# Second block's output projection as seven block products, its two weight tiles released one after the other

## The reference, cut to what matters

```python
mixed = concatenate([rms_norm(out_a, ...), rms_norm(out_b, ...), rms_norm(out_c, ...)], axis=-1)
x = x + einsum('bsc,cd->bsd', mixed, w_out)              # 256x1024 by 1024x1024
x = x + expert_choice_moe(rms_norm(x, norm_ffn), w_router, b_router, w_gate, w_up, w_down)
...
# expert_choice_moe
logits = einsum('bsd,de->bse', x, w_router) + b_router
aff = softmax(logits)
gate, idx = top_k(aff.transpose(0, 2, 1), cap)
xs = x[bidx, idx]
hid = silu(einsum('becd,edf->becf', xs, w_gate)) * einsum('becd,edf->becf', xs, w_up)
ys = einsum('becf,efd->becd', hid, w_down) * gate
```

## Time and profile before

| | us |
|---|---|
| median of 3 runs | 1926.46 (1926.03 to 1927.03) |
| the profiled execution | 1926.92 |
| its span, first to last instruction | 1925.1 |
| PE busy | 1643.8 (85%) |
| DVE / ACT / POOL busy | 764.6 / 313.8 / 182.2 |
| bytes read from HBM | 594.76 MB |

### The profile page before, as it was taken

How to read it: one execution, slowest core, us unless ns; L and a number is a source line. 1 busy time by engine, 2 the same in 40 slices (tenths; PEclk the granted TensorE clock), 3 DMA queues, 4 the chain that set the end, 5 groups by cost and what they waited for, 6 DMA issues and landing times.

```text
span 1925.1 us, 25329 instructions
## 1 busy us (share of the span) xinstructions
PE 1643.8 (85%) x10768; PEld 941.6 (49%) x10768; DVE 764.6 (40%) x1502; ACT 313.8 (16%) x823; POOL 182.2 (9%) x175
## 2 busy tenths in 40 slices
PE   8999999999999999999776766757999785756757
PEld 3455999444589964574332232322474432232322
DVE  1586788877738886663010100102573010010101
ACT  1243111021521101262000000001252000010000
POOL 0001034000215410310000000000210000000000
PEclk9999999999999999999897987879999897897978
DMA  9992998434454743546999999999746999999998
GB/s 356 330 355 91 330 334 279 153 131 175 135 189 169 263 153 125 184 181 274 415 432 428 427 434 423 434 428 402 243 175 255 403 428 432 425 434 425 432 429 351
DMA packets 165960, 599.81 MB, mean 312 GB/s; under 512 B 20976, under 2 KB 79856, under 8 KB 142064
## 3 DMA queue, kind: packets, MB, share of 16 engines
q1 hardware_dynamic: 165630, 598.04, 79.2%
q10 hardware_dynamic: 242, 0.53, 0.1%
HBM read 594.76 MB, written 3.80 MB: 311 GB/s over the span
## 4 chain that ended last, share of the span: by engine, by line
PE 55%; DMA 38%; DVE 4%; ACT 2%; issue 1%; POOL 0%; SPq 0%; DVEq 0%; ACTq 0%; POOLq 0%
DMA extra<-in_w_down 14%; DMA extra<-in_w_up 13%; DMA extra<-in_w_gate 11%; PE ps L1393 7%; PE ps L1420 7%; PE ps L1747 5%; PE ps L1347 5%; PE ps L1018 4%; PE ps L1187 4%; PE ps L1464 4%; PE ps L1629 3%; PE ps L1289 3%; PE ps L1495 2%; PE ps L1767 1%; DVE extra L2548 1%
## 5 line engine op out<-in xcount | busy, mean ns | idle before, releaser
L1747 PE MATMUL ps<-ring,wide 128*32 128x256 f32 x2912 | 226.2, 478 | 123.9 <-DMA ring<-in_w_up 79.4
L1747 PEld LDWEIGHTS ps<-ring,wide 128*32 128x32 f32 x2912 | 109.5, 136 | 233.9 <-DMA ring<-in_w_up 89.0
L3446 DVE TENSOR_TENSOR wide<-ps,wide 128x512 f32<-128x512 f32 x16 | 10.7, 670 | 506.1 <-PE ps L1747 506.1
L1767 PE MATMUL ps<-ring,wide 128*32 128x512 f32 x768 | 158.4, 641 | 47.7 <-DMA ring<-in_w_down 44.0
L1747 PE MATMUL ps<-extra,wide 128*32 128x256 f32 x1056 | 87.1, 499 | 55.9 <-DMA extra<-in_w_up 31.8
L1767 PEld LDWEIGHTS ps<-ring,wide 128*32 128x32 f32 x768 | 42.2, 117 | 159.8 <-issue 127.6
L1393 PE MATMUL ps<-hT,ring 128*128 128x128 f32 x960 | 114.7, 275 | 0.0
L1393 PEld LDWEIGHTS ps<-hT,ring 128*128 128x128 f32 x960 | 111.0, 192 | 1.0 <-issue 1.0
L1347 PE MATMUL ps<-hT,ring 128*128 128x128 f32 (+1 forms) x704 | 100.2, 304 | 0.0
L2315 ACT ACTIVATE wide<-ps 128x512 f32<-128x512 f32 x8 | 4.8, 597 | 566.5 <-PE ps L1767 425.3
L1347 PEld LDWEIGHTS ps<-hT,ring 128*128 128x128 f32 x704 | 94.0, 191 | 5.8 <-issue 1.0
(11 more groups left out here) (399 smaller groups left out, 2364.5 us busy)
## 6 DMA issues: line engine op xcount, KB each, us to landing
ring<-in_w_gate SPq DMA_DIRECT2D x24, 4096.0 KB, 31.3
ring<-in_w_down SPq DMA_DIRECT2D x24, 4096.0 KB, 33.2
ring<-in_w_up SPq DMA_DIRECT2D x20, 4096.0 KB, 32.7
ring<-in_w_mod SPq DMA_DIRECT2D x24, 2048.0 KB, 12.9
ring<-in_w_up SPq DMA_DIRECT2D x44, 1024.0 KB, 9.5
extra<-in_w_gate SPq DMA_DIRECT2D x8, 4096.0 KB, 35.1
extra<-in_w_up SPq DMA_DIRECT2D x8, 4096.0 KB, 33.0
ring<-in_w_in SPq DMA_DIRECT2D x13, 2048.0 KB, 9.8
```

Of the source, the lines that this page charges most:

```text
L1747: last = mm(ps[2 * part + e // 2][j * CAP:(j + 1) * CAP, e % 2 * 2 * P:(e % 2 + 1) * 2 * P], xsT[:, k, e * CAP:(e + 1) * CAP], expert_row( ...
L1767: last = mm(ps[6 + n][e * CAP:(e + 1) * CAP, :], hidT[:, e, k, :], expert_row(n0, e, k)[:, n * N:(n + 1) * N], start=k == 0, stop=k == KD - 1)
```

## The change: what it does

The product `mixed @ w_out` is cut in two by rows (`c`), by the inner dimension (`e`, four of the eight chunks each) and by columns (`n`). Eight products of such blocks become seven, of four matmuls each: `block_out(m)`, in the order 1, 7, 2, 6, 3, 5, 4. For them DVE forms four sums of row blocks (`rows3`: s1 to s4, 512 elements a row) and four of weight blocks in place (`weights3`: t1 to t4, 2048 elements a row), and adds the products into `x` in more steps (`product_add`, `shared_add`). ACT copies product 1 once into `out2_u`. The rows of `w_out` are laid in another order in memory outside of the launch, to match `h8`. The far scale moves: DVE scales `proj2` itself (`far_scale`) ahead of the far transposes, and PE waits for that (`b2_mixed_ready`, 2). Row chunk 1 of `x` is now completed right half first. The weight tiles change places, ("out", 1) comes first; it is released by the first matmul of product 5, ("out", 0) by the last of product 4. The pair in their place is loaded as two halves (`pair_half`), each behind its own tile.

```diff
+OUT2_STEPS = (1, 7, 2, 6, 3, 5, 4)
+OUT2_BANK = {1: 4, 7: 5, 2: 2, 6: 0, 3: 1, 5: 3, 4: 6}
+OUT2_SUMS = ("s3", "t3", "t2", "s1", "s2", "s4", "t4", "t1")
+OUT2_NEEDS = {1: (), 7: ("s3", "t3"), 2: (), 6: ("s2", "t2"), 3: ("s4",), 5: ("s1", "t1"), 4: ("t4",)}
...
-B2_TILES = [("in", i) for i in range(5)] + [("small", 0), ("out", 0), ("out", 1)]
+B2_TILES = [("in", i) for i in range(5)] + [("small", 0), ("out", 1), ("out", 0)]
...
-                sp.wait_ge(tile_done, b2_used(L, 7))
-                pair(3)
+                for h in range(2):
+                    sp.wait_ge(tile_done, b2_used(L, SLOTS + h))
+                    pair_half(G_PAIRS - 1, h)
...
+                def block_out(m, some=range(4)):
+
+                    if some[0] == 0:
+                        for name in OUT2_NEEDS[m]:
+                            pe.wait_ge(*out2_sum(s, name))
+                    w, h = out2_weights(), out2_rows()
+                    lhs, rhs = {1: (h[0][0], w[0][0]), 2: (h[0][1], w[1][0]), 3: (h[0][1], w[1][1]), 4: (h[1][1], w[1][0]),
+                                5: (h[1][0], w[0][0]), 6: (h[0][0], w[0][0]), 7: (out2_s3, w[0][1])}[m]
+                    for g in some:
+                        last = mm(ps[OUT2_BANK[m]][:, :], lhs[:, g, :], rhs[:, g, :], start=g == 0, stop=g == 3)
+                        if m == 5 and g == 0:
+                            last.then_inc(tile_done, 1)
+                    if some[-1] == 3:
+                        if m == 4:
+                            last.then_inc(tile_done, 1)
+                        else:
+                            last.then_inc(s.up("block_product_done"), 1)
...
+                block_out(1)
+                block_out(7, range(0, 2))
+                pe.wait_ge(*s.at("b2_mixed_ready", 2))
                 for i, (_, _, col) in enumerate(FAR):
                     for c in range(2):
                         o = ((i + 1) % 2) * T + c * P
                         last = nc.tensor.transpose(ps[6 + (i + 1) // 2][:, o:o + P], proj2[:, c, col:col + P], ident)
                     if i in (0, 2):
                         last.then_inc(s.up("b2_out_flipped"), 1)
-                out2(5, NEAR, 0, 1).then_inc(s.up("b2_out_done"), 1)
-                out2(0, NEAR, 1, 0).then_inc(s.up("b2_out_done"), 1)
-                out2(1, NEAR, 1, 1).then_inc(s.up("b2_out_done"), 1)
+                block_out(7, range(2, 4))
+                pe.wait_ge(*s.at("b2_proj_by_act", 7))
                 pe.wait_ge(*s.at("b2_out_by_act", 3))
                 pe.wait_ge(*s.at("b2_out_by_dve", 2))
-                out2(2, FAR, 0, 0).then_inc(s.up("b2_out_done"), 1)
-                out2(3, FAR, 0, 1).then_inc(s.up("b2_out_done"), 1)
+                block_out(2)
+                block_out(6)
+                block_out(3)
...
-                out2(6, FAR, 1, 0, slice(0, 2))
-                flip_rows(0)
-                out2(6, FAR, 1, 0, slice(2, 3)).then_inc(tile_done, 1)
-                out2(7, FAR, 1, 1, slice(0, 2))
+                flip_rows(0, (0,))
+                block_out(5)
+                block_out(4, range(0, 2))
+                flip_rows(0, (1,))
+                block_out(4, range(2, 4))
                 pe.wait_ge(sems["router_loaded"], 16 + DEPTH)
                 pe.wait_ge(sems["pads_cleared"], 4)
                 pe.wait_ge(*s.at("b2_x_by_act", 3))
                 pe.wait_ge(*s.at("b2_x_by_dve", 3))
                 route(0).then_inc(s.up("b2_router_done"), 1)
-                out2(7, FAR, 1, 1, slice(2, 3)).then_inc(tile_done, 1)
+                flip_rows(1, (1,))
+                logits(0)
                 flip_rows(1, (0,))
-                logits(0)
-                flip_rows(1, (1,))
+                pe.wait_ge(*s.at("b2_x_by_act", 4))
+                route(1, range(4, KD), 1)
                 pe.wait_ge(*s.at("b2_x_by_dve", 4))
-                route(1, range(0, 4))
-                pe.wait_ge(*s.at("b2_x_by_act", 4))
-                route(1, range(4, KD)).then_inc(s.up("b2_router_done"), 1)
+                route(1, range(0, 4), 1).then_inc(s.up("b2_router_done"), 1)
...
+                act.wait_ge(*out2_done(s, L, 1))
+                av(out2_u, ps[OUT2_BANK[1]][:, :], ACT.Copy).then_inc(s.up("b2_proj_by_act"), 1)
...
+                def far_scale():
+
+                    dve.wait_ge(*s.at("b2_mixed_rstd", 2))
+                    for c in range(2):
+                        v = proj2[:, c, CQ2:CQ2 + 384]
+                        ts(v, v, rsm[1][:, 3 * c + 2:3 * c + 3], None, ALU.mult)\
+                            .then_inc(s.up("b2_mixed_ready" if c else None), 1)
+
+                def rows3(name):
+
+                    if name == "s3":
+                        dve.wait_ge(*s.at("b2_out_by_act", 2))
+                    elif name == "s1":
+                        dve.wait_ge(*s.at("b2_out_by_act", 3))
                     else:
-                        dve.wait_ge(tile_done, b2_used(L, B2_AT[("out", n)]))
-                    xv = x[:, c, n * N:(n + 1) * N]
-                    stt(xv, ps[2 + 4 * c + n][:, :], rsm[1][:, 3 * c + 2:3 * c + 3], xv, ALU.mult, ALU.add)\
-                        .then_inc(s.up("b2_mixer_added"), 1)
+                        dve.wait_ge(*out2_done(s, L, {"s2": 1, "s4": 2}[name]))
+                    dve.wait_ge(*s.own())
+                    out_, p, q, op = {"s3": (out2_s3, h[0][0], h[1][0], ALU.subtract), "s1": (h[1][0], h[1][0], h[1][1], ALU.add),
+                                      "s2": (h[0][0], h[1][0], h[0][0], ALU.subtract),
+                                      "s4": (h[0][1], h[0][1], h[0][0], ALU.subtract)}[name]
+                    tt(out_, p, q, op).then_inc(s.up("block_sum_ready"), 1)
+
+                def weights3(name):
+
+                    if name == "t3":
+                        for n in range(2):
+                            dve.wait_ge(*b2_loaded(L, B2_AT[("out", n)]))
+                    else:
+                        dve.wait_ge(*out2_done(s, L, {"t2": 1, "t4": 2, "t1": 6}[name]))
+                        dve.wait_ge(*out2_sum(s, {"t2": "t3", "t4": "t2", "t1": "t4"}[name]))
+                    out_, p, q, op = {"t3": (w[0][1], w[1][1], w[0][1], ALU.subtract), "t2": (w[0][0], w[0][1], w[0][0], ALU.add),
+                                      "t4": (w[1][0], w[0][0], w[1][0], ALU.subtract),
+                                      "t1": (w[0][0], w[1][1], w[0][0], ALU.subtract)}[name]
+                    tt(out_, p, q, op).then_inc(s.up("block_sum_ready"), 1)
+
+                def product_add(m, c, n, name=None, op=ALU.add):
+
+                    dve.wait_ge(*out2_done(s, L, m))
+                    dve.wait_ge(*s.own())
+                    tt(xh[c][n], xh[c][n], ps[OUT2_BANK[m]][:, :], op).then_inc(s.up(name), 1)
+
+                def shared_add():
+
+                    dve.wait_ge(*out2_done(s, L, 6))
+                    dve.wait_ge(*s.at("b2_proj_by_act", 7))
+                    tt(out2_u, out2_u, ps[OUT2_BANK[6]][:, :], ALU.add).then_inc(s.up(), 1)
+                    dve.wait_ge(*s.own())
+                    for c, n in ((0, 1), (1, 1), (1, 0)):
+                        tt(xh[c][n], xh[c][n], out2_u, ALU.add).then_inc(s.up(), 1)
...
-                near_add(0, 0)
+                rows3("s3")
+                weights3("t3")
+                far_scale()
+                weights3("t2")
                 dve.wait_ge(*s.at("b2_out_flipped", 4))
                 gained(FAR[0:1], 6, T, "b2_out_by_dve")
-                near_add(0, 1)
-                near_add(1, 0)
-                near_add(1, 1)
-                dve.wait_ge(*s.at("b2_mixed_rstd", 2))
-                dve.wait_ge(*s.own())
-                far_add(0, 0)
-                far_add(0, 1)
+                rows3("s1")
+                rows3("s2")
+                product_add(1, 0, 0)
+                product_add(7, 1, 1)
+                product_add(7, 1, 0)
+                rows3("s4")
+                product_add(2, 0, 0, "b2_mixer_added")
+                weights3("t4")
+                weights3("t1")
+                shared_add()
+                product_add(3, 0, 1)
+                product_add(5, 0, 1, "b2_mixer_added")
+                product_add(5, 1, 1, "b2_mixer_added")
                 ffn_mean(0)
                 evac_rows(0)
-                far_add(1, 0)
-                far_add(1, 1)
+                product_add(4, 1, 0, "b2_mixer_added", ALU.subtract)
```

More of the change, by code:

```diff
@@ L579, in in2_done, with out2_weights, out2_rows, out2_done @@
             return s.at("block_product_done", IN2_STEPS.index(m) + 1)
+        def out2_weights():
+            v = [slot2(B2_AT[("out", n)]).rearrange("p (e g m) -> p e g m", e=2, g=4) for n in range(2)]
+            return [[v[n][:, e, :, :] for n in range(2)] for e in range(2)]
+        def out2_rows():
+            v = hT[:, :].rearrange("p (e g c t) -> p e c g t", e=2, g=4, c=2)
+            return [[v[:, e, c, :, :] for e in range(2)] for c in range(2)]
```

(10 more changed lines are left out.)

53 lines of the change are left out of this document (24 added, 29 removed).

## The result

| | before | after |
|---|---|---|
| median of the runs, us | 1926.46 (1926.03 to 1927.66) | 1917.45 (1914.68 to 1917.87) |
| ratio, 95% interval | | 0.995 (0.9937 to 0.9964) |
| profiled execution, us | 1926.92 | 1917.87 |
| way, layer 1 / 2 | 57.22 / 57.21 | 54.51 / 54.49 |
| stage, layer 1 / 2 | 526.23 / 415.26 | 523.63 / 413.65 |

A forecast was written before the change was run, and what follows sets the result against it. The prediction took PE's path from first output product to first expert product as what decides the end. 3.43 - 0.45 - 0.25 - 0.15 = 2.6 us a layer, 5.2 in two, gave 1921.3 us, range 1919.3 to 1923.8.

The forecast's parts named there:

- the way: PE's path from first output product to first expert product, which releases the row parts: 2.6 us shorter a layer.
- Four matmuls fewer at 0.858: Output projection on PE: 32 matmuls become 28, saving 3.43 us a layer.
- POOL held by t3: Root for the far scaling: POOL's first operation waits for weight sum t3, taking about 1.6 to 1.7 us.
- Its price on PE: PE waits caused by the late root: 0.45 us at the far transposes, 0.25 at product 2.
- the second router copy: End of the output projection: 3.4 us from product 4's end to this copy, against 3.26 before; 0.15 lost.
- From there on the end is fixed: bytes left over rate: Expert weight stream after the row parts and following pairs are issued: its remaining time was taken as fixed.
- I price this at nothing: Earlier release of pair(3)'s halves, 2 MB into the stream's hole: no gain, at most some 0.6 us a layer.
- The thin moment: DMA queues thin at 1493, share 0.59: removing this might bring some 0.6 us a layer.
- POOL gets through: Rival at the far scaling's root: POOL is not held, losses 0.45 and 0.25 go, 1919.9 us; chance 0.17.
- The halves bring 2 MB where they count: Rival on pair(3)'s halves or the thin queues: 0.6 us a layer more gain, 1920.1 us; chance 0.06.
- The half-eaten gain: Rival: longer hand-overs between DVE, ACT and PE cost 0.9 us more a layer, 1923.1 us; chance 0.15.
- DVE as the bound: Rival: weight sums stretch to 3.68 us beside POOL, making each layer 2.0 us slower, 1930.5 us; chance 0.04.

The follow-up runs named there:

- e3: Changed kernel with four useless matmuls added behind product 4, which put PE's count back to 32; 1923.58 us, ratio to before 0.9994.
- e4: Changed kernel with weight sum t3 moved ahead of DVE's read-out of the last input projection piece; 1914.95 us, ratio to before 0.9943.
- e8: Kernel before with pair(3) issued only behind the router's second product; 1924.7 us, ratio to before 0.9996.
- e12: Changed kernel with pair(3) as one transfer, issued only when the router's second product is done; 1919.61 us, ratio to before 0.9969.
- e13: Changed kernel with pair(3) as one transfer, issued only when the router's first product is done; 1919.55 us, ratio to before 0.9969.
- e6: Changed kernel with pair(3) as one transfer, issued behind the last transposes of x; 1916.26 us, ratio to before 0.9953.
- e1: Changed kernel with pair(3) as one 4 MB transfer again, behind both output tiles; 1916.52 us, ratio to before 0.9955.
- e5: Kernel before with only the two halves of pair(3) added, each behind its own tile; 1922.05 us, ratio to before 0.9981.
- e7: Changed kernel with t3 moved ahead of the last input projection read-out and pair(3) as one transfer behind both tiles; 1915.19 us, ratio to before 0.9944.
- e14: Kernel before with pair(3) in two halves, both issued where it issues the whole pair; 1925.45 us, ratio to before 0.9995.
- e2: Changed kernel with both halves of pair(3) issued behind the second output tile; 1916.71 us, ratio to before 0.9952.

## Why the sign was right and the size wrong

**Right: the way.** Each term can be held against the traces.
- Four matmuls fewer at 0.858: e3 puts four back for 3.41 a layer.
- POOL held by t3: predicted 1.6 to 1.7 and an end with t3, measured 1.68 and 0.05 behind it. The Trainium skill (SBUF — State Buffer, "Who interferes with whom") says that a VectorE instruction with two SBUF inputs contends with a GpSimd instruction that reads SBUF. The trace agrees, 0.20 to 1.68, and e4 shows the way back.
- Its price on PE: predicted 0.45 and 0.25 for the copy behind it (t2 is laid 0.1 too short there: 5.6 + 2.29 is 7.9), measured 0.28 and 0.09 (1449.93 to 1450.02 in the chain). Yet taking t3 away brought 0.84, more than these two. The chains of after and of e4 account for it: the transposes end at T + 6.54 and at T + 6.04 (0.50, of which 0.28 is marked as idle), product 2 follows 0.09 later, and the twelve matmuls from there on take 10.54 for 10.30 (in e4 fourteen take 12.02), 0.24 in which no idle row shows where. In all 0.83, for 0.70 predicted. I had taken too much from the idle row and too little from what stands behind it.
- Behind it: t1 0.8 before its use (predicted 1.0), last product's end at T + 26.63 (predicted 26.3), from there to the second router copy 3.34 (predicted 3.4; 1471.64 - 1468.30).
- Sum: 2.72 a layer for the predicted 2.6, in both layers.

**Wrong: "From there on the end is fixed: bytes left over rate", and with it that the change is worth what it takes off the way "and nothing else".** The sum has no term for a shorter stage, and what pair(3)'s release could bring stands there as "I price this at nothing", with a bound of 0.6 a layer. That term was mis-sized: the stage is 1.9 a layer shorter. The stages of before have a mean of 525.45 and 415.53 over three profiles, those of after 523.50 and 413.61 over two: 1.95 and 1.92. With the way, 5.4 + 3.9 = 9.3 against 9.0 measured. The first sentence can stand; what I did not do is count the bytes left and ask whether the change alters them. I took the share of 1.01 at 1495 for the stream's full rate, while the same row says 381 GB/s. The packets of before leave 0.53 and 0.60 MB more 4 us behind the way (means of its three profiles against the two of after). At the 430 GB/s or so of the stage (429 from 1500 to 1880 in the profile after) that is an estimated 1.2 and 1.4 us, most of the 1.9; in layer 2, 1.6 are there when 185 MB have landed and the rest comes in the last 0.6 MB, unexplained.

The table shows where these bytes are from, in two ways. With pair(3) 12.3 to 12.5 us ahead of the row parts, 1.7 MB of it are left there, too much to be caught up (e8, e12). At 15.0 us only 0.7 MB are left, but the packets that follow take 0.173 to 0.191 instead of 0.160 to 0.170, and the loss is the same (before, e13). Between them, at 13.7, with 1.2 MB left, there is none (e6), and at 15.6 or with 2 MB early there is none either (e1, after, e5). The kernel before stood on one of the bad places. The change takes it off, by the earlier halves and also without them, since its output tiles are free 15.6 us ahead of the row parts instead of 15.0. That is why leaving the halves out costs nothing in e1 and e7, why they bring 3.7 in e5, and why e13, which only puts the old distance back, loses 3.0. That the halves are in the change was no merit of the forecast either: without them (e1) the gain is the same. The thin moment (0.59 at 1493) was close to the right place, but not the cost itself: the first packets behind it are as slow in the changed kernel. My bound held the missing bytes of that one microsecond and not those of the six behind it.

**The rivals.** That POOL gets through did not come about, though e4 shows that its price was fair: 0.84 a layer on the way, where 0.70 was given. "The halves bring 2 MB where they count" named the right object with a price of 0.6 and a chance of 0.06. The half-eaten gain and DVE as the bound are refuted by the PE and DVE rows of after: no idle PE from product 2 to product 4, and no sum over 2.34.

**Open.** Why packets of 4 KB are slow at a distance of 15.0 and not at 13.7 or 15.6 is not settled. In the slow cases the last 8 KB packets ahead of the row parts end 0.7 to 1.8 us behind the start of the first 4 KB one, but in e1, e6 and e7 they do so too (0.7 to 2.3), so this overlap alone doesn't explain it. Layer 2 of e14, issued at 15.0 and 14.6, has no slow packets, and layer 2 of e2 and of e7 lies between the two groups (0.170 and 0.169) with little more left behind the way (10.39 and 10.42). Between 13.7 and 15.0 no whole pair was tried.

## What to carry to other kernels

Where a stage ends on a stream, count two things at the point where it becomes full: the bytes still to land, and the GB/s beside the share. A full share is no rate. A change that only moves a release by half a microsecond can take a transfer off or onto a bad place, which here was worth 1.9 us a layer beside the 2.7 for which the change was made; test it by moving that one issue in both kernels. And look for the long two-input sum that stands beside a short POOL operation on the path: moving it to an idle gap brought 0.84 us a layer for nothing.

## What the runs showed of the hardware

- At the same DMA share (0.99 to 1.03), packets of 4 KB moved 351 to 381 GB/s in some stretches (before, e13) and 401 to 419 in others (after, e6, e12), and took 0.173 to 0.191 against 0.160 to 0.165 us each. Moving the issue of the transfer ahead of them by 0.6 us (e13 against e1) switched between the two.
- A backlog of 1.2 MB at the start of that stretch cost nothing in the median (e6), one of 1.7 MB cost 1.1 to 1.7 us a layer in the stage (e12 against e1, e8 against e5).
- The same program took from 1922.6 to 1929.9 where it stood on the bad place, and the variants off it spread over 1.7 to 4.7 us. The program up to T of layer 1 took 861.5 to 863.9 over sixteen profiles.
- A GpSimd operation of 0.20 us took 1.68 beside a VectorE sum with two SBUF inputs, and 0.20 again without it (e4).
